# Two 128-column matmuls of a weight tile become one 256-column matmul in four blocks, and 8 more places get it

## The chip, the cores and the metric

The kernel runs on one NeuronCore of a Trainium2 chip. The metric is the device time of one execution in microseconds (us). Three runs of the kernel before took 982.0, 982.35 and 982.47 us, median 982.35 us. All tensors are float32. Five engines work side by side: TensorE (PE, matmuls, with its weight loads listed apart as PEld), VectorE (DVE), ScalarE (ACT), GpSimd (POOL) and SyncE (SP), which issues the DMAs.

## The reference

Three transformer layers on 256 tokens of width 1024: a latent-attention layer (0) and a chunked-attention layer (1), each with a SwiGLU feed-forward of width 2816, then a gated block with two attentions and a convolved feed-forward (2). Cut to what matters here:

```
for layer 0, 1:
    y = mixer(rms_norm(x))            # q, k, v products, softmax, @ w_o
    x = x + rms_norm(y)
    h = rms_norm(x)
    f = (silu(h @ w_gate) * (h @ w_up)) @ w_down
    x = x + rms_norm(f)
layer 2:
    proj = modulate(rms_norm(x)) @ w_in      # q, k, v of two attentions, gates
    mixed = (g_a * (oa @ w_br_moba) + g_b * (ob @ w_br_sb)) @ w_out
    x = x + gt_m * mixed
    u = conv(modulate(rms_norm(x)) @ w_up)
    x = x + gt_f * ((gelu(u_gate) * u_val) @ w_down)
    return rms_norm(x)
```

## The kernel before, in words

**Products.** Activations lie transposed: feature chunk k of 128 rows, 256 tokens as columns. Each 128x128 weight tile is multiplied with a 128x256 activation chunk. For accuracy every float32 operand is split into a high and a low part, both of type fp32r, and a product is three matmuls into the same 128x256 half of a PSUM bank: high weights by high activations (line 508), high weights by low activations (line 509), low weights by high activations (line 514). Each matmul is preceded on PE by the load of its own 128x128 weights. In `lead` (lines 528, 529, 535), which starts a stage while its activations are still being made, the high activations go first and the low ones after them.

**Weights.** SP brings pieces of 16 tiles (1 MB) into four buffers `raw`. ACT copies a piece to its high part `whi` (line 906), DVE subtracts that from the original and gives the low part `wlo` (line 1382). There are three `whi`/`wlo` buffers. PE's `weight` waits for the low part of a piece before its first use.

**Order.** Each engine's order is written out by hand as a program of its own; semaphores tie them. The stages are those of `STREAM`: `wa`, the latent products (`mla`), `wo0`, `gu0`, `dn0`, `wkv_v`, `wkv_k`, `wq1`, `wo1`, `gu1`, `dn1`, `win_v`, `win_k`, `win_q`, `win_g`, `wbr`, `wout`, `up2`, `dn2`. `gu` is gate and up of a feed-forward, `dn` its down product. `tiles` computes two output chunks at a time, n and n+1, over all k. Between stages lie the norms, which go through PE (sums of squares by a matmul with ones), ACT (logarithm, exponential) and DVE.

**The halved places.** At 29 places the third matmul of a product (line 514) is two matmuls of 128 columns instead (lines 511 and 512), each with its own load of the same weights. The table `HALVED` says where: in `tiles`, at k = 1 of chunk n, when n divides by the number in the table; and at k = 1 of the first chunk of each `dn` stage. That is 5 places each in `gu0`, `gu1` and `up2`, 4 in each `dn`, one in `wkv_k` and one in `win_k`.

Of the kernel before, what the change touches and what calls it, by code (L numbers as in the profile page):

```python
# [13 lines left out]
T = 256  # L14
P = 128
# [83 lines left out]
def _used_up(name, t):  # L99
# [3 lines left out]

AFTER = {"exp": ("scores", 5), "scale": ("exp", 4), "values": ("turn1", 3), "chunk": ("values", 2),
         "keep": ("sticks", 9), "sums": ("keep", 8), "stick": ("sums", 4)}
HALVED = {"gu0": 8, "gu1": 8, "up2": 8, "dn0": 2, "dn1": 2, "dn2": 2, "wkv_k": 8, "win_k": 8}
FREE = ("scale", "exp", "chunk", "keep", "stick")


# [196 lines left out]
def build(nc, a):  # L306
    ctx = ExitStack()
    with ctx:
# [177 lines left out]
        def tensor_program(e, counted):  # L486
# [10 lines left out]
            def weight(name, t, n=1):  # L497
# [4 lines left out]
                s, at = w % SPLIT, slice(c * P, (c + n) * P)  # L502
                return whi[s][:, at], wlo[s][:, at], w if c + n == PIECES[WEIGHTS[w]][3] else None

            def product(name, t, out, xh, xl, k, first, last, event=None, halves=False):

                hi, lo, used = weight(name, t)
                e.matmul(out, hi, xh[:, k, :], start=first, stop=False, skip_group_check=True)  # L508
                e.matmul(out, hi, xl[:, k, :], start=False, stop=False, skip_group_check=True)  # L509
                if halves:  # L510
                    e.matmul(out[:, 0:P], lo, xh[:, k, 0:P], start=False, stop=last, skip_group_check=True)
                    m = e.matmul(out[:, P:T], lo, xh[:, k, P:T], start=False, stop=last, skip_group_check=True)
                else:
                    m = e.matmul(out, lo, xh[:, k, :], start=False, stop=last, skip_group_check=True)  # L514
                if used is not None or event is not None:
                    m.then_inc(S.gemm.tick(("used", used), event), 1)

            def lead(name, m, nk, xh, xl, made, bs, by):

                for i, b in enumerate(bs):  # L520
                    take(b, by, (name, 2 * i))
                    bank_of[name, 2 * i] = b
                for k in range(nk):
                    q.wait_ge(S.xhi, (made, k))
                    for j in range(m):
                        out = banks[bs[j // 2]][:, (j % 2) * T:(j % 2 + 1) * T]
                        hi, lo, _ = weight(name, k * m + j)
                        e.matmul(out, hi, xh[:, k, :], start=k == 0 and j % 2 == 0, stop=False, skip_group_check=True)  # L528
                        e.matmul(out, lo, xh[:, k, :], start=False, stop=False, skip_group_check=True)  # L529
                    q.wait_ge(S.xlo, (made, k))  # L530
                    for j in range(m):
                        out = banks[bs[j // 2]][:, (j % 2) * T:(j % 2 + 1) * T]
                        hi, lo, used = weight(name, k * m + j)
                        event = (name, j - 1) if k == nk - 1 and j % 2 == 1 else None
                        last = e.matmul(out, hi, xl[:, k, :], start=False, stop=k == nk - 1, skip_group_check=True)  # L535
                        if used is not None or event is not None:
                            last.then_inc(S.gemm.tick(("used", used), event), 1)

            def tiles(name, n, m, nk, xh, xl, made, b, by, last=0, seven=None):


                out = take(b, by, (name, n + last))
                outs = [out[:, j * T:(j + 1) * T] for j in range(m)]
                bank_of[name, n] = b
                if seven is not None:
                    outs[1] = take(seven, by, (name, n + last))[:, 0:T]
                    bank_of[name, "seven"] = seven
                for j in range(m):
                    for k in range(nk):
                        q.wait_ge(S.xlo, (made, k))  # L550
                        event = (name, n) if j == m - 1 else (name, "six") if seven is not None else None
                        product(name, (n + j) * nk + k, outs[j], xh, xl, k, k == 0, k == nk - 1,
                                event if k == nk - 1 else None, name in HALVED and j == 0 and k == 1 and n % HALVED[name] == 0)

            def token_block(name, g, nk, xh, xl, k, tb):

# [111 lines left out]
            def out_chunk(name, t, xh, xl, made):  # L668

                k, j = t // 8, t % 8  # L670
                if k == 0 and j % 2 == 0:
                    take(j // 2, S.resid, (name, j + 1))
                    bank_of[name, j] = j // 2
                q.wait_ge(S.xlo, (made, "o", k))
                product(name, t, banks[j // 2][:, (j % 2) * T:(j % 2 + 1) * T], xh, xl, k, k == 0 and j % 2 == 0, k == 7,
                        (name, j - 1) if k == 7 and j % 2 == 1 else None)


            q.wait_ge(S.const, "ones")
# [133 lines left out]
            for step, i in _order2():  # L813
                if step in ("win_q", "win_g"):
                    n, k = i // 8, i % 8
                    if n % 2 == 0 and k == 0:
                        bank_of[step, n] = n // 2 % 3
                        take(n // 2 % 3, S.act_out, (step, n))
                    q.wait_ge(S.xlo, ("h4", k))
                    product(step, i, banks[n // 2 % 3][:, (n % 2) * T:(n % 2 + 1) * T], hh, hl, k, k == 0, k == 7,  # L820
                            (step, n - 1) if n % 2 == 1 and k == 7 else None)
                elif step == "scores":
                    q.wait_ge(S.act_out, ("win_k", i // 2 * 2))
                    q.wait_ge(S.act_out, ("win_q", i // 2 * 2))
                    scores("o2", i, half_parts(A2, i), (3, 4))
                elif step == "turn":
                    turn("o2", A2, *i, (5, 6)[i[1]])
                elif step == "sticks":
                    q.wait_ge(S.act_out, ("win_k", i // 2 * 2))
                    q.wait_ge(S.act_out, ("win_q", i // 2 * 2))  # L830
                    (heads,) = half_parts(A2, i)
                    pair_banks = []
                    for a in range(2):
                        b = 3 + 2 * (i % 2) + a
                        pair_banks.append(take(b, S.dve_tmp, ("least", i, a)))
                        bank_of["sticks", i, a] = b
                    for a, (x, y) in enumerate(heads):
                        e.matmul(pair_banks[a][:, 0:T], y[:, 0:P], x, start=True, stop=True, skip_group_check=True)
                    for a, (x, y) in enumerate(heads):
                        e.matmul(pair_banks[a][:, T:384], y[:, P:T], x[:, P:T], start=False, stop=True,  # L840
                                 skip_group_check=True).then_inc(S.attn.tick(("sticks", i, a)), 1)
                elif step == "sums":
                    for a in range(2):
                        bank, r = banks[bank_of["sticks", i, a]], A2.PT[i % 2][:, a, :]
                        q.wait_ge(S.past, ("keep", i, a))
                        e.matmul(bank[:, 0:T], tri[:, :], r[:, 0:T], start=False, stop=False, skip_group_check=True)
                        e.matmul(bank[:, P:T], negones[:, :], r[:, T:384], start=False, stop=False,
                                 skip_group_check=True)
                        e.matmul(bank[:, T:384], tri[:, :], r[:, T:384], start=False, stop=True,
                                 skip_group_check=True).then_inc(S.attn.tick(("sums", i, a)), 1)  # L850
                elif step == "values" and i < 4:
                    values("o2", A2, i, 64, A2.PT[i % 2], ("win_v", 0, 1), S.soft, ("o2", "turned", i, 1), 7)
                elif step == "values":
                    values("o2", A2, i, 64, A2.S[i % 2], ("win_v", 1, 1), S.past, ("stick", i, 1), 7)


            for n in range(8):
                bank_of["wbr", n] = (0, 1, 2, 3, 6, 7, 0, 1)[n]
                bank = take(bank_of["wbr", n], S.dve_tmp, ("gated", n))
                for b in range(2):  # L860
                    for k in range(4):
                        q.wait_ge(S.xlo, ("o2", "o", 4 * b + k))
                        product("wbr", n * 8 + b * 4 + k, bank[:, b * T:(b + 1) * T], A2.oh[:, 4 * b:4 * b + 4, :],
                                A2.ol[:, 4 * b:4 * b + 4, :], k, k == 0, k == 3,
                                ("wbr", n) if b == 1 and k == 3 else None)
            lead("wout", 4, 8, hh, hl, "mix", (4, 5), S.resid)
            for n in (4, 6):
                tiles("wout", n, 2, 8, hh, hl, "mix", (6, 7)[n // 2 - 2], S.resid, seven=3 if n == 6 else None)
# [1288 lines left out]
```

## Time and profile before

| | |
|---|---|
| median of three runs | 982.35 us (982.0 to 982.47) |
| span of the profiled execution, first to last instruction | 980.3 us |
| median above that span | 2.05 us |
| PE busy with matmuls | 958.4 us, 98% |
| PE busy with weight loads | 923.9 us, 94% |
| DVE busy | 720.6 us, 74% |
| ACT busy | 542.4 us, 55% |
| granted TensorE clock, mean over the span | 0.999 |
| HBM traffic | 197 GB/s over the span |

The page gives the span of the profiled execution and no device time of its own beside it; what lies around the span is read from the median of the other runs. A matmul is pipelined: its listed length (some 276 ns) is from the start of its reading to its modelled end, and the next one starts long before that. So the pace of PE is the distance from one start to the next, which the timeline gives to 10 ns and a window row gives as a mean: the window's length plus one matmul's length, divided by the count of matmuls that touch the window.

### The profile page before, as it was taken

Reading aid. Unit: us, or ns where it says so; the run is one execution under the profiler, and the core shown is the slowest. Engines: PE = TensorE matmul, PEld = TensorE weight load, DVE = VectorE, ACT = ScalarE, POOL = GpSimd, SP = SyncE. Lnnn points to the kernel's source line nnn. Section 1 sums busy time; section 2 is a strip of 40 time slices with the busy share of each in tenths; the row PEclk is TensorE's granted clock in tenths of the full one; section 3 lists DMA queues with packets and bytes.
Section 4 is the critical chain, followed back from the end, with each engine's and each line's share of the span. In section 5 each row is a group of like instructions: output and inputs, shape, how many; then the busy total and the mean of one; then the engine's idle time right before and its main releaser. Section 6 shows DMA issues by size and latency. Waiting matters only on the chain.

```text
span 980.3 us, 18888 instructions
## 1 busy us (share of the span) xinstructions
PE 958.4 (98%) x7971; PEld 923.9 (94%) x7971; DVE 720.6 (74%) x1340; ACT 542.4 (55%) x837; POOL 25.4 (3%) x54
## 2 busy tenths in 40 slices
PE   8999999999999999999999999999999999999997
PEld 8889999999998988899999997998999999999996
DVE  7965897777658777698879788555654879888653
ACT  7554664454447366565444545456755567666542
POOL 0300000000000000000000000000220000000000
PEclk9999999999999999999999999999999999999999
DMA  8536376766744734368767882653343545555621
GB/s 298 190 116 238 128 266 255 255 251 225 295 172 168 266 129 140 116 212 304 265 251 267 331 315 76 245 185 116 111 149 132 199 157 207 181 203 184 216 87 43
DMA packets 27588, 194.72 MB, mean 199 GB/s; under 512 B 3056, under 2 KB 3184, under 8 KB 4592
## 3 DMA queue, kind: packets, MB, share of 16 engines
q1 hardware_dynamic: 27504, 193.51, 54.7%
q8 instruction: 63, 1.03, 0.4%
q14 instruction: 21, 0.17, 0.0%
HBM read 192.45 MB, written 1.05 MB: 197 GB/s over the span
## 4 chain that ended last, share of the span: by engine, by line
PE 89%; ACT 4%; DVE 4%; issue 2%; DMA 1%; POOL 0%; SPq 0%; DVEq 0%; ACTq 0%
PE bank L508 25%; PE bank L509 24%; PE bank L514 23%; PE bank L639 2%; PE bank L665 2%; PE bank L569 2%; PE bank L563 2%; ACT s_whi L906 2%; PE bank L564 2%; PE bank L528 2%; PE bank L535 1%; PE bank L529 1%; PE bank L649 1%; DVE s_wlo L1382 1%; DMA s_xT<-in_xT 1%
## 5 line engine op out<-in xcount | busy, mean ns | idle before, releaser
L1382 DVE TENSOR_TENSOR s_wlo<-s_raw,s_whi 128x512 fp32r<-128x512 f32 (+1 forms) x364 | 372.3, 1065 | 138.1 <-ACT s_whi L906 137.9
L906 ACT ACTIVATE s_whi<-s_raw 128x1024 fp32r<-128x1024 f32 (+2 forms) x233 | 304.8, 1335 | 215.6 <-PE bank L514 205.9
L508 PE MATMUL bank<-s_hh,s_whi 128*128 128x256 f32 x1400 | 393.6, 281 | 1.1 <-DVE s_wlo L1382 0.7
L509 PE MATMUL bank<-s_hl,s_whi 128*128 128x256 f32 x1400 | 387.6, 277 | 0.0
L514 PE MATMUL bank<-s_hh,s_wlo 128*128 128x256 f32 x1383 | 382.8, 277 | 0.0
L508 PEld LDWEIGHTS bank<-s_hh,s_whi 128*128 128x128 f32 x1400 | 263.3, 188 | 6.9 <-issue 5.9
L509 PEld LDWEIGHTS bank<-s_hl,s_whi 128*128 128x128 f32 x1400 | 263.2, 188 | 0.1
L514 PEld LDWEIGHTS bank<-s_hh,s_wlo 128*128 128x128 f32 x1383 | 259.8, 188 | 0.0
L508 PE MATMUL bank<-s_ph,s_whi 128*128 128x256 f32 x528 | 146.4, 277 | 0.0
L509 PE MATMUL bank<-s_pl,s_whi 128*128 128x256 f32 x528 | 145.8, 276 | 0.0
L514 PE MATMUL bank<-s_ph,s_wlo 128*128 128x256 f32 x516 | 142.5, 276 | 0.0
L509 PEld LDWEIGHTS bank<-s_pl,s_whi 128*128 128x128 f32 x528 | 99.2, 188 | 0.0
L508 PEld LDWEIGHTS bank<-s_ph,s_whi 128*128 128x128 f32 x528 | 99.2, 188 | 0.0
L514 PEld LDWEIGHTS bank<-s_ph,s_wlo 128*128 128x128 f32 x516 | 96.9, 188 | 0.0
L1397 DVE CUSTOM_DVE_ANT_0 s_raw<-s_raw,s_adacc 128x1024 f32<-128x1024 f32 x48 | 56.7, 1219 | 0.0
L528 PE MATMUL bank<-s_hh,s_whi 128*128 128x256 f32 x160 | 39.8, 284 | 5.3 <-DVE s_wlo L1382 3.1
L529 PE MATMUL bank<-s_hh,s_wlo 128*128 128x256 f32 x160 | 39.1, 279 | 0.0
L508 PE MATMUL bank<-s_oh,s_whi 128*128 128x256 f32 x128 | 36.9, 288 | 0.6 <-DVE s_ol L1464 0.4
L1647 DVE TENSOR_TENSOR s_tmp<-bank,s_R 128x256 f32<-128x256 f32 x44 | 18.6, 422 | 25.3 <-PE bank L514 22.0
L528 PEld LDWEIGHTS bank<-s_hh,s_whi 128*128 128x128 f32 x160 | 30.2, 189 | 6.6 <-ACT s_hh L1022 2.2
L509 PE MATMUL bank<-s_ol,s_whi 128*128 128x256 f32 x128 | 35.8, 280 | 0.0
L514 PE MATMUL bank<-s_oh,s_wlo 128*128 128x256 f32 x128 | 35.8, 280 | 0.0
(238 smaller groups left out, 1285.3 us busy)
## 6 DMA issues: line engine op xcount, KB each, us to landing
s_raw<-in_gu SPq DMA_DIRECT2D x44, 1024.0 KB, 4.9
s_raw<-in_dn SPq DMA_DIRECT2D x33, 1024.0 KB, 4.9
s_raw<-in_wada SPq DMA_DIRECT2D x24, 1024.0 KB, 5.7
s_raw<-in_up SPq DMA_DIRECT2D x22, 1024.0 KB, 4.9
s_raw<-in_wo SPq DMA_DIRECT2D x8, 1024.0 KB, 4.9
s_raw<-in_win_g SPq DMA_DIRECT2D x8, 1024.0 KB, 4.9
s_raw<-in_mla SPq DMA_DIRECT2D x4, 1024.0 KB, 5.4
s_raw<-in_wkv_v SPq DMA_DIRECT2D x4, 1024.0 KB, 4.9
```

The lines of the kernel that those rows point to most:

```text
L508: e.matmul(out, hi, xh[:, k, :], start=first, stop=False, skip_group_check=True)
L509: e.matmul(out, hi, xl[:, k, :], start=False, stop=False, skip_group_check=True)
L514: m = e.matmul(out, lo, xh[:, k, :], start=False, stop=last, skip_group_check=True)
L528: e.matmul(out, hi, xh[:, k, :], start=k == 0 and j % 2 == 0, stop=False, skip_group_check=True)
L529: e.matmul(out, lo, xh[:, k, :], start=False, stop=False, skip_group_check=True)
L563: e.matmul(out, xh[:, k, xk], hi, start=k == 0, stop=False)
L564: e.matmul(out, xh[:, k, xk], lo, start=False, stop=False)
L569: m = e.matmul(out, xl[:, k, xk], hi, start=False, stop=k == nk - 1)
L639: m = e.matmul(pair_banks[a][:, cols_], x[:, blk * P:(blk + 1) * P], y[:, 0:rows], start=i == 0 and blk == 0, stop=last, skip_group_check= ...
L906: e.activation(whi[w % SPLIT][:, at], raw[p % RAW][:, at], ACT.Copy).then_inc(S.hi.tick((w, c0)), 1)
L1382: e.tensor_tensor(wlo[s][:, at], raw[p % RAW][:, at], whi[s][:, at].bitcast(F32), ALU.subtract).then_inc(S.lo.tick((i, j), (i, "all")), 1)
L1397: m = e.tensor_tensor_reduce(out=src, in0=src, in1=cact[:, :], scale=1.0, scalar=0.0, op0=ALU.mult, op1=ALU.add, accum_out=modv[:, j:j + 1])
```

## The change

It alters the matmuls of PE alone; no semaphore, DMA or instruction of another engine is added, removed or moved.

- At the 29 places the two 128-column matmuls become one matmul over all 256 columns. Its source (activations) and its target (PSUM) are both read through `turned_order`: 64 columns at a time, block 0, block 2, block 1, block 3. Every column still gets its own sum.
- Eight places are added that had one plain matmul: chunk n = 10 of `gu0`; weight tile 36 of `wo0`, 52 of `wo1`, 96 of `win_g`, 49 of `wbr`; and k = 1, j = 0 of the three leads of `gu1`, `wout` and `up2`, where the matmul with the low weights is the second one.

```
-HALVED = {"gu0": 8, "gu1": 8, "up2": 8, "dn0": 2, "dn1": 2, "dn2": 2, "wkv_k": 8, "win_k": 8}
+HALVED = {"gu0": (8, 10, 16, 24, 32, 40), "gu1": (8, 16, 24, 32, 40), "up2": (8, 16, 24, 32, 40),
+          "dn0": (0, 2, 4, 6), "dn1": (0, 2, 4, 6), "dn2": (0, 2, 4, 6), "wkv_k": (0,), "win_k": (0,)}
+HALVED_UNIT = {"wo0": (36,), "wo1": (52,), "win_g": (96,), "wbr": (49,)}
+HALVED_LEAD = ("gu1", "wout", "up2")
...
+            def turned_order(ap):
+
+                return ap.rearrange("p (a b c) -> p b a c", a=2, b=2)
...
                 if halves:
-                    e.matmul(out[:, 0:P], lo, xh[:, k, 0:P], start=False, stop=last, skip_group_check=True)
-                    m = e.matmul(out[:, P:T], lo, xh[:, k, P:T], start=False, stop=last, skip_group_check=True)
+                    m = e.matmul(turned_order(out), lo, turned_order(xh[:, k, :]), start=False, stop=last, skip_group_check=True)
...
-                        e.matmul(out, lo, xh[:, k, :], start=False, stop=False, skip_group_check=True)
+                        if name in HALVED_LEAD and k == 1 and j == 0:
+                            e.matmul(turned_order(out), lo, turned_order(xh[:, k, :]), start=False, stop=False,
+                                     skip_group_check=True)
+                        else:
+                            e.matmul(out, lo, xh[:, k, :], start=False, stop=False, skip_group_check=True)
...
-                                event if k == nk - 1 else None, name in HALVED and j == 0 and k == 1 and n % HALVED[name] == 0)
+                                event if k == nk - 1 else None, j == 0 and k == 1 and n in HALVED.get(name, ()))
```

On PE, in `gu0` at chunk n = 16 (152.2 us in the trace), before: `whi` and `wlo` are the weight parts, `hh` and `hl` the activation parts.

```order
970 L508 MATMUL bank1<-s_hh,s_whi0 128x256
971 L509 MATMUL bank1<-s_hl,s_whi0 128x256
972 L511 MATMUL bank1<-s_hh,s_wlo0 128x128
973 L512 MATMUL bank1<-s_hh,s_wlo0 128x128
974 L508 MATMUL bank1<-s_hh,s_whi0 128x256
975 L509 MATMUL bank1<-s_hl,s_whi0 128x256
976 L514 MATMUL bank1<-s_hh,s_wlo0 128x256
```

The same place on PE in the changed kernel:

```order
969 L515 MATMUL bank1<-s_hh,s_whi0 128x256
970 L516 MATMUL bank1<-s_hl,s_whi0 128x256
971 L518 MATMUL bank1<-s_hh,s_wlo0 128x2x2x64
972 L515 MATMUL bank1<-s_hh,s_whi0 128x256
973 L516 MATMUL bank1<-s_hl,s_whi0 128x256
974 L520 MATMUL bank1<-s_hh,s_wlo0 128x256
```

Two rows became one of a new form, 128x2x2x64; with it one weight load goes.

On PE, in the lead of `up2` at k = 1 (791.6 us in the trace), before:

```order
5830 L535 MATMUL bank2<-s_hl,s_whi0 128x256 x2
5831 L528 MATMUL bank1<-s_hh,s_whi0 128x256
5832 L529 MATMUL bank1<-s_hh,s_wlo0 128x256
5833 L528 MATMUL bank1<-s_hh,s_whi0 128x256
5834 L529 MATMUL bank1<-s_hh,s_wlo0 128x256
```

The same place on PE in the changed kernel:

```order
5810 L545 MATMUL bank2<-s_hl,s_whi0 128x256 x2
5811 L534 MATMUL bank1<-s_hh,s_whi0 128x256
5812 L536 MATMUL bank1<-s_hh,s_wlo0 128x2x2x64
5813 L534 MATMUL bank1<-s_hh,s_whi0 128x256
5814 L539 MATMUL bank1<-s_hh,s_wlo0 128x256
```

Here the count stays the same and one matmul takes the new form.

## Rows read from the trace of the kernel before

**Rows 1.** The page: span and busy times, then the chain that ended last.

```profile
span 980.3 us, 18888 instructions
PE 958.4 (98%) x7971; PEld 923.9 (94%) x7971; DVE 720.6 (74%) x1340; ACT 542.4 (55%) x837; POOL 25.4 (3%) x54
...
PE 89%; ACT 4%; DVE 4%; issue 2%; DMA 1%; POOL 0%; SPq 0%; DVEq 0%; ACTq 0%
```

**Rows 2.** Stretches of PE: window, its us, PE busy (count), clock, DMA share, GB/s.

```profile
91.20:100.90 9.70, 9.70 (x84) 1.00 1.00 391
135.30:152.10 16.80, 16.80 (x145) 1.00 0.90 320
401.30:405.10 3.80, 3.80 (x34) 1.00 0.00 0
411.80:427.10 15.30, 15.30 (x132) 1.00 0.32 112
791.60:813.20 21.60, 21.60 (x186) 1.00 0.43 157
153.30:174.00 20.70, 20.70 (x185) 1.00 0.65 235
435.30:456.30 21.00, 21.00 (x188) 1.00 0.90 318
152.70:289.00 136.30, 136.30 (x1203) 1.00 0.67 240
813.60:971.80 158.20, 158.20 (x1395) 1.00 0.46 161
316.90:346.10 29.20, 29.20 (x258) 1.00 0.75 281
434.80:592.80 158.00, 158.00 (x1395) 1.00 0.79 286
625.40:653.00 27.60, 27.60 (x245) 1.00 0.54 194
```

**Rows 3.** Timeline of PE around one halved place: start us, length us.

```profile
174.10 0.22 PE L511 MATMUL bank<-s_hh,s_wlo 128*128 128x128 f32 x1
174.16 0.28 PE L512 MATMUL bank<-s_hh,s_wlo 128*128 128x128 f32 x1
174.27 0.33 PE L508 MATMUL bank<-s_hh,s_whi 128*128 128x256 f32 x1
174.44 0.28 PE L509 MATMUL bank<-s_hl,s_whi 128*128 128x256 f32 x1
...
175.02 0.28 PE L508 MATMUL bank<-s_hh,s_whi 128*128 128x256 f32 x1
```

**Rows 4.** Timeline of DVE and PE at the end of the `gu1` lead.

```profile
426.07 2.28 DVE L1382 TENSOR_TENSOR s_wlo<-s_raw,s_whi 128x2048 fp32r<-128x2048 f32 x1
...
428.50 0.36 PE L508 MATMUL bank<-s_hh,s_whi 128*128 128x256 f32 x1 [0.67 <-DVE s_wlo L1382]
```

**Rows 5.** Timeline of ACT, DVE and PE in the `wbr` and `wout` stages.

```profile
756.45 0.36 PE L508 MATMUL bank<-s_oh,s_whi 128*128 128x256 f32 x1
...
757.67 0.42 ACT L1287 ACTIVATE s_hh<-s_tmp 128x256 fp32r<-128x256 f32 x1 [3.39 <-DVE s_tmp L1882]
757.99 1.90 ACT L906 ACTIVATE s_whi<-s_raw 128x2048 fp32r<-128x2048 f32 x1
...
754.01 2.29 DVE L1382 TENSOR_TENSOR s_wlo<-s_raw,s_whi 128x2048 fp32r<-128x2048 f32 x1 [0.96 <-ACT s_whi L906]
759.92 2.29 DVE L1382 TENSOR_TENSOR s_wlo<-s_raw,s_whi 128x2048 fp32r<-128x2048 f32 x1 [0.96 <-ACT s_whi L906]
765.84 2.29 DVE L1382 TENSOR_TENSOR s_wlo<-s_raw,s_whi 128x2048 fp32r<-128x2048 f32 x1 [0.95 <-ACT s_whi L906]
```

**Rows 6.** Timeline of DVE and PE in `gu0`, then at the start of `up2`.

```profile
132.17 2.28 DVE L1382 TENSOR_TENSOR s_wlo<-s_raw,s_whi 128x2048 fp32r<-128x2048 f32 x1
...
134.60 0.36 PE L508 MATMUL bank<-s_hh,s_whi 128*128 128x256 f32 x1
...
148.60 2.28 DVE L1382 TENSOR_TENSOR s_wlo<-s_raw,s_whi 128x2048 fp32r<-128x2048 f32 x1
...
157.22 0.28 PE L508 MATMUL bank<-s_hh,s_whi 128*128 128x256 f32 x1
...
797.13 4.50 DVE L1382 TENSOR_TENSOR s_wlo<-s_raw,s_whi 128x2048 fp32r<-128x2048 f32 x2 [1.32 <-ACT s_whi L906]
...
801.36 0.28 PE L508 MATMUL bank<-s_hh,s_whi 128*128 128x256 f32 x1
```

More of the change, by code:

```diff
@@ L675, in out_chunk @@
                 product(name, t, banks[j // 2][:, (j % 2) * T:(j % 2 + 1) * T], xh, xl, k, k == 0 and j % 2 == 0, k == 7,
-                        (name, j - 1) if k == 7 and j % 2 == 1 else None)
+                        (name, j - 1) if k == 7 and j % 2 == 1 else None, t in HALVED_UNIT[name])
             q.wait_ge(S.const, "ones")
@@ L820, in tensor_program @@
                     product(step, i, banks[n // 2 % 3][:, (n % 2) * T:(n % 2 + 1) * T], hh, hl, k, k == 0, k == 7,
-                            (step, n - 1) if n % 2 == 1 and k == 7 else None)
+                            (step, n - 1) if n % 2 == 1 and k == 7 else None, i in HALVED_UNIT.get(step, ()))
                 elif step == "scores":
@@ L864, in tensor_program @@
                                 A2.ol[:, 4 * b:4 * b + 4, :], k, k == 0, k == 3,
-                                ("wbr", n) if b == 1 and k == 3 else None)
+                                ("wbr", n) if b == 1 and k == 3 else None, n * 8 + b * 4 + k in HALVED_UNIT["wbr"])
             lead("wout", 4, 8, hh, hl, "mix", (4, 5), S.resid)
```

## The prediction

> **What bounds the kernel now.** I read the page first. PE is busy for 98% of the span and makes up 89% of the chain that ended last [rows 1], so the question is at what pace PE works. Its listed busy time cannot say that, since each matmul is listed with its whole pipelined length. I therefore asked for windows inside long runs without a wait, and took the distance from start to start: the window's length plus one matmul's length (0.28 us), over the count.
>
> Two paces come out [rows 2]. Window 153.30 to 174.00: (20.70 + 0.28) / 185 = 113.4 ns a matmul; 435.30 to 456.30: 21.28 / 188 = 113.2. Window 135.30 to 152.10: 17.08 / 145 = 117.8 ns; 791.60 to 813.20: 21.88 / 186 = 117.6; 411.80 to 427.10: 15.58 / 132 = 118.0. The instructions are of the same form, the granted clock is 1.00 (2.4 GHz) in all of them, and the DMA share does not separate them (0.90 and 0.43 at the slow pace, 0.65 and 0.90 at the fast). So PE has a fast pace of 113.4 ns and a slow one of 117.8, 4.4 ns or 4% apart, and keeps whichever it has. The slow one is entered after waits, and left at a wait or at a halved place: the window of `gu0` up to 152.10 is slow, the one behind its halved place is fast. This is what the timeline allows me to say; why a pace holds it doesn't show.
>
> The other engines bound only the starts of stages, where PE waits for a low weight part or for a norm.
>
> **The change part by part.**
>
> *1. The second matmul and its weight load go, at 29 places.* In a fast stretch the halved place runs from 174.10 to 175.02, 0.92 us for 8 steps [rows 3]. Without the extra matmul there would be 7 steps of 113.4 ns, 0.794 us. A halved place thus costs 0.126 us: one whole step of 113 ns, for a matmul costs a step whether it has 128 or 256 columns, and 13 ns in the five steps behind it, from 174.44 to 175.02 (5 steps in 0.58 against 0.567 us). The one at 129.4 us stands ahead of a wait: DVE's low part ends at 134.45 and PE goes on at 134.60 [rows 6], so its gain is lost there. 28 x 0.126 = 3.5 us.
>
> *2. What the new form costs by itself.* The trace has no matmul in blocks of 64. From below: nothing; it has 256 columns and one weight load, like its neighbours at 113.4 ns, and doing less than these is excluded, as the same count of columns is read. From above: the 0.126 us of the halved place, which also breaks the run of columns and loads weights twice. I take the small disturbance seen behind the halved place, 13 ns, because the nearest row is the plain 256-column matmul and a break in a run of columns is what the halved place has in common with the new form. It counts at 28 old and 5 new places: 33 x 0.013 = 0.4 us.
>
> The row first: the two-part place shows that breaking 256 columns once costs 13 ns beside the extra step. The Trainium skill ("Advanced Engine Details and Errata", section "PSUM Cachelines") says that any non-contiguous access pattern slows matmuls significantly, and that pairs of elements should be contiguous for best throughput. By its first sentence part 1 would give back most of what it gains; by its second a pattern that breaks only every 64 elements costs next to nothing. It gives no figure, and no row here decides; the rival of a dear form below is what its first sentence would make here.
>
> *3. The pace behind the eight new places.* If the new form resets the pace as the halved place did, the slow stretch behind each becomes fast. By the windows there stand behind them [rows 2]: `wo0` 9.98 / 0.1178, 84 touched, 82 whole; `gu0` 143; `wo1` 32; lead of `up2` 183. Together 440 x 4.4 ns = 1.94 us. The first two and the last end in work of PE or in a norm that hangs on PE's last sum, so this gain reaches the end. Weights are there: in `gu0` the part ready at 150.88 is used at 157.22; in `up2` the one ready by 801.63 is the later of two, and the first of them, ready by about 799.4, is used at 801.36 [rows 6].
>
> The lead of `gu1` has 130 slow matmuls, 0.57 us, but behind it PE waits 0.67 us for a low part that DVE ends at 428.35 after its own run of norm work [rows 4]. PE would wait longer: nothing gained. In `wbr` and `wout` the slow steps are covered too: DVE's low parts come every 5.91 us (754.01, 759.92, 765.84), in a ring of DVE and ACT that doesn't pass through PE (low part, DVE's mix, ACT's copy at 757.67, high part at 757.99, next low part) [rows 5], while PE needs 48 x 0.1178 = 5.65 us for a piece even when slow. Nothing gained. Tile 96 of `win_g` comes at about 727 us, eight matmuls ahead of the next attention step, and is counted at nothing.
>
> *4. The pace at the old places.* 24 of the 29 stand in fast stretches, where only part 1 matters. Of the others three stand in slow ones with a long run behind: `gu0` at 152.2, `wkv_k` at 316.6, `up2` at 813.3. If the new form resets there too, nothing changes.
>
> Sum: -3.5 + 0.4 - 1.9 = -5.0 us. The profiled execution's span of 980.3 us would be 975.3; with the 2.05 us between span and median of the runs, 977.3 us. What becomes late next: nothing in the feed-forward stages, where low parts are ready some 5 us ahead; at the starts of stages the waits for low parts stay where they are.
>
> **The rivals.**
>
> *The new form doesn't reset the pace* (the side of slower). It runs like a plain matmul, with one weight load after the other, and the two quick 128-column steps (174.10 to 174.16) that may be what shifts the pace are gone. Then the slow stretches run on: from 152.70, from 813.60 and from 316.90 the windows touch 1203 + 1395 + 258 = 2856 matmuls, less 16 second halves and some 10 at the edges 2830 [rows 2]. 2830 x 4.4 ns = 12.5 us, against 29 x 0.126 = 3.6 saved: +8.9, 991.2 us. It decides from 3600 / 4.4 = 820 slow matmuls on. For it: every step out of the slow pace that I see was a halved place or a wait. Against it: the pace is left after disturbances of different kinds (a wait, the sums of a norm), so it seems to take little.
>
> *It resets, but is dear.* If one new-form matmul costs as much as the halved place, the old places gain nothing and the five useful new ones cost 0.6: 982.35 - 1.9 + 0.6 = 981.0 us.
>
> *It also throws PE from the fast pace into the slow one.* Then the stretches from 434.80 and 625.40 turn slow as well, some 1640 more matmuls [rows 2], 4470 in all: 19.7 - 3.6 = +16.1, 998.4 us. For it: a disturbance by a wait ends in either pace. Against it: all halved places in fast stretches ended fast.
>
> *The paces are dealt anew.* All waits shift by fractions of a us, and each can end in either pace; stretches with no place in them (before `wo0`, `wq1`, `win_g` from 730 to 750 us with some 170 matmuls) may turn slow or fast, 0.7 us apiece. If this or a later wait for DVE takes half of the gain: about 980 us.
>
> **How the numbers follow.** 0.64 for the forecast (977.3, own range 974.8 to 979.6), 0.12 for the dear form, 0.12 for no reset, 0.04 for the throw into the slow pace, 0.08 for half the gain. A gap of 0.2% (2.0 us) is about what a measurement of this kernel can tell from no change, so faster means below 980.4, slower above 984.3. Faster: nearly all of the forecast's 0.64, over half of the 0.08 and a quarter of the dear form (0.126 us is its upper end), 0.71. Same: the rest of these, 0.13. Slower: no reset and the throw, 0.16. The range from 974.6 to 983.0 holds the forecast, the dear form and the half gain, 0.8 together; no reset stays outside.
>
> **What would show it.** The page: 29 matmuls fewer, 7942. The timeline of PE at 152 us: after the new form the next starts come at 0.11 to 0.12 us with no 0.17 step, and the windows behind it give 113.4 ns. The windows after the new places in `wo0`, `gu0`, `wo1` and the lead of `up2` give 113.4 and not 117.8. The wait of PE for the low part after the lead of `gu1` grows from 0.67 to about 1.2 us, and the distance of low parts in `wout` stays at 5.91. I am wrong if windows behind a new-form matmul give 117.8, or if the step at that matmul is much over 0.13 us.

## The result, and the profile after

The changed kernel took 992.33 us (median of four runs: 987.30, 991.61, 993.04, 998.16), the kernel before 982.41 us (982.0 to 985.99) beside it. The ratio is 1.0096, 95% interval 1.0072 to 1.0119: slower by 1%, where 977.3 us and faster had been forecast. The rival "no reset" had 991.2 us. The spread of the four runs, 11 us, is part of the result.

The profile below is of the slowest of the four, 998.16 us, so it shows the loss at its largest. The page of the changed kernel, the lines that answer to [rows 1]:

```profile
span 994.4 us, 18830 instructions
PE 971.9 (98%) x7942; PEld 937.4 (94%) x7942; DVE 720.8 (72%) x1340; ACT 542.1 (55%) x837; POOL 25.4 (3%) x54
...
PE 92%; DVE 3%; ACT 3%; issue 1%; DMA 1%; POOL 0%; SPq 0%; DVEq 0%; ACTq 0%
```

The 29 matmuls and weight loads are gone, PE's listed busy time is 13.5 us longer all the same, and the other engines do the same work in the same time. So the matmuls that are left go at another pace. The windows of PE (window, its us, busy and count, clock, DMA share, GB/s), which answer to [rows 2]:

```profile
91.20:100.90 9.70, 9.70 (x83) 1.00 1.02 391
135.30:152.10 16.80, 16.80 (x145) 1.00 0.92 319
153.30:174.00 20.70, 20.70 (x178) 1.00 0.65 235
152.70:289.00 136.30, 136.30 (x1160) 1.00 0.66 237
320.90:346.10 25.20, 25.20 (x225) 1.00 0.77 287
404.90:409.00 4.10, 4.10 (x37) 1.00 0.00 0
434.80:600.00 165.20, 165.20 (x1405) 1.00 0.77 278
801.00:822.00 21.00, 21.00 (x181) 1.00 0.42 153
813.60:971.80 158.20, 158.20 (x1346) 1.00 0.49 172
```

Window 153.30 to 174.00 now holds 178 matmuls instead of 185: (20.70 + 0.28) / 178 = 117.9 ns, the slow pace, behind the place that had ended it. The windows 152.70 to 289.00, 434.80 to 600.00 and 813.60 to 971.80 give 117.7, 117.8 and 117.7 ns: the three long stretches, `gu0` with `dn0`, `gu1` with `dn1`, `up2` with `dn2`, are slow from end to end. In the kernel before, the second of them was fast from its start, and the other two from the halved places at 152.2 and 813.3 us on. The short stretches in `wo0`, `wo1` and the lead of `up2` are slow as well, 120.2, 118.4 and 117.6 ns (the first two windows are so short that an edge counts). Of the stretches shown only `wkv_k`, 320.90 to 346.10, is fast, 113.2 ns.

PE around the turned matmul at chunk n = 16 of `gu0`, the place shown in the order above (start us, length us), which answers to [rows 3]:

```profile
152.00 0.28 PE L516 MATMUL bank<-s_hl,s_whi 128*128 128x256 f32 x1
152.12 0.28 PE L518 MATMUL bank<-s_hh,s_wlo 128*128 128x256 f32 x1
152.24 0.28 PE L515 MATMUL bank<-s_hh,s_whi 128*128 128x256 f32 x1
152.36 0.28 PE L516 MATMUL bank<-s_hl,s_whi 128*128 128x256 f32 x1
152.47 0.28 PE L520 MATMUL bank<-s_hh,s_wlo 128*128 128x256 f32 x1
```

Line 518 starts 0.12 us after its neighbour and the next one 0.12 us after it. In this trace the turned matmul does nothing: it costs nothing and changes nothing. PE comes to 31 of the 37 places at the slow pace and leaves each of them at the slow pace; it comes to the other six fast, or going over to fast, and leaves them fast.

I counted the slow steps in both traces: of some 7000 distances of 105 to 126 ns from one start to the next, taken in groups of up to nine, about 1160 go at the slow pace in the kernel before and about 5030 in the changed one. That is 3870 x 4.4 ns = 17.0 us more, less 29 x 0.126 = 3.7 us for the matmuls taken out, and PE's idle time (span less busy time, 22.5 against 21.9 us) is 0.6 us longer: +13.9 us. The two spans are 14.1 us apart (994.4 - 980.3).

### The profile page after: what moved, and what is told of

It reads as the page before. It is cut to its first block, busy times and chain, and to the rows that moved or that the text cites. A ratio compares the mean times of both kernels' runs of the same rounds, so it can differ in the third digit from the quotient of the medians.

```text
span 994.4 us, 18830 instructions
## 1 busy us (share of the span) xinstructions
PE 971.9 (98%) x7942; PEld 937.4 (94%) x7942; DVE 720.8 (72%) x1340; ACT 542.1 (55%) x837; POOL 25.4 (3%) x54
## 4 chain that ended last, share of the span: by engine, by line
PE 92%; DVE 3%; ACT 3%; issue 1%; DMA 1%; POOL 0%; SPq 0%; DVEq 0%; ACTq 0%
PE bank L515 25%; PE bank L516 25%; PE bank L520 24%; PE bank L649 2%; PE bank L675 2%; PE bank L534 2%; PE bank L579 2%; PE bank L545 2%; PE bank L573 2%; PE bank L574 2%; PE bank L539 2%; PE bank L659 1%; ACT s_whi L916 1%; DVE s_wlo L1392 1%; DMA s_xT<-in_xT 1%
## 5 line engine op out<-in xcount | busy, mean ns | idle before, releaser
L516 PE MATMUL bank<-s_hl,s_whi 128*128 128x256 f32 x1400 | 391.9, 280 | 0.0
L516 PE MATMUL bank<-s_pl,s_whi 128*128 128x256 f32 x528 | 148.5, 281 | 0.0
L515 PE MATMUL bank<-s_ph,s_whi 128*128 128x256 f32 x528 | 148.5, 281 | 0.0
L520 PE MATMUL bank<-s_ph,s_wlo 128*128 128x256 f32 x516 | 145.1, 281 | 0.0
L1943 DVE SCALAR_TENSOR_TENSOR s_tmp<-bank,s_cols,s_tmp 128x255 f32<-128x255 f32 (+1 forms) x44 | 21.2, 482 | 20.5 <-ACT s_tmp L1336 19.7
```

The lines of the kernel that those rows point to most:

```text
L1943: e.scalar_tensor_tensor(out=v[:, shift:T], in0=bank[:, 0:T - shift], scalar=col(name, n), in1=v[:, shift:T], op0=ALU.mult, op1=ALU.add)
```

## The experiments

Theory from here on: a wait deals the pace, fast or slow, anew in each execution; PE keeps it until the next wait, or other work of PE such as a norm's sums or attention, or until a halved place; and the turned form is a plain matmul. Rivals: the turned form itself, or the eight new places, make PE slow. The first four kernels ran on one chip beside the kernel before (982.99 us there), the last four on another (983.84 us). Each time below is the median of all runs of a kernel; a ratio is given where the times are tight.

**The halved form at all 37 places.** The change's list of places with the old form:

```
-                    m = e.matmul(turned_order(out), lo, turned_order(xh[:, k, :]), ...)
+                    e.matmul(out[:, 0:P], lo, xh[:, k, 0:P], ...)
+                    m = e.matmul(out[:, P:T], lo, xh[:, k, P:T], ...)
```

> The changed kernel with the old form at all 37 places: two matmuls of 128 columns instead of one in four blocks. Theory (the turned form does nothing; only the halved form takes PE out of the slow pace): the stretches of gu0, gu1, the dn stages and up2 run at 113.4 ns again, all halved places cost 0.126 us, and the eight new ones end the slow stretches behind them in wo0, gu0, wo1 and the up2 lead: 982.4 + 8 x 0.126 - 1.9, about 981.4 us (980.5 to 982.5). Rival (the slower time of the changed kernel comes from the eight new places, wherever they stand): it stays at 987 us or more.

982.8 us (981.21 to 983.67, 11 runs), ratio 0.9994 (0.9986 to 1.0003): no change from before, and tight. So the eight new places do no harm; the form is what differs. It had been expected 0.9 us under the kernel before (1.9 saved, 1.0 spent) and is 0.2 us under it. My reading, which no run tests by itself: the stretches that were slow in the profile before are not all slow in every execution, so ending them is worth less on average, and eight more places cost 1.0 us always. The ten profiles of this case bear it out in part. Ahead of their places, `wo0` and `wo1` were slow in all ten, `gu0` in five, the lead of `up2` in three. Weighted so, the 440 matmuls give (82 + 32 + 143/2 + 183 x 0.3) x 4.4 ns, an estimate of 1.1 us saved for 1.0 spent.

**No turned and no halved form.** All tables empty, and none in the `dn` stages.

```
+HALVED = {}
+HALVED_UNIT = {"wo0": (), "wo1": (), "win_g": (), "wbr": ()}
+HALVED_LEAD = ()
```

> The changed kernel with plain 256-column matmuls at all 37 places: no turned and no halved form anywhere. Theory (turned is the same as plain): the same times as the changed kernel, 987 to 998 us with the same wide spread from run to run, and slow stretches of over a thousand matmuls at 117.8 ns. Rival (the turned form itself slows PE or keeps it slow): 978.8 us, the kernel before less 29 x 0.126 us, and tight.

986.45 us, 12 runs: 979.14, 979.25, 980.03, 980.29, 980.65; 986.15, 986.75, 987.52, 987.60; 991.42, 993.16; 999.95. The times come in steps. The run that was profiled took 979.14 us, and its three long stretches were all fast (windows, columns as above):

```profile
137.00:287.00 150.00, 150.00 (x1326) 1.00 0.71 254
430.00:590.00 160.00, 160.00 (x1414) 1.00 0.80 289
790.00:967.00 177.00, 177.00 (x1564) 1.00 0.48 165
```

That is 113.3, 113.4 and 113.4 ns over more than 1300, 1400 and 1500 matmuls without any halved place: a pace holds by itself. A slow draw costs 1343 x 4.4 = 5.9 us in the first, 1439 x 4.4 = 6.3 in the second, 1583 x 4.4 = 7.0 in the third. No slow stretch is 979 to 981, one is 985 to 988, two are 991 to 993, three 998 to 1000: the steps that were measured. The same code gave both 979 and 1000 us. The granted clock doesn't tell the runs apart: its mean over the span was 0.996 in the fastest and in the slowest.

Not every stop deals anew, though: `wo0` and `wo1`, which follow an attention stage, start slow in all ten profiles, `win_g` behind its last attention step in nine. The long stretches are the ones that come out either way.

**The turned form at the 29 old places alone.** `HALVED` with the chunks of the kernel before, the other two tables empty.

> The turned form at the 29 old places alone, plain at the eight new ones. Theory: as the changed kernel, 987 to 998 us. Rival (the new places do the harm): below the kernel before, 978.8 us.

987.02 us, 12 runs: 979.55, 980.11, 982.92; 985.43, 985.93, 986.66, 987.39; 990.53, 991.45, 992.64; 998.59, 999.51. The same ladder; the run of 982.92 us is the profiled one, with the three long stretches fast and, among the slow short ones, `win_k` and the lead of `gu0`, which the kernel before had fast. In that profile too no turned place changes the pace. The rival that the turned form makes PE slow falls, as three runs are as fast as the plain kernel's best; the rival that the new places do so falls too.

**The halved form at 8 places, each just behind a wait.**

```
+HALVED = {"gu0": (10,), "gu1": (6,), "wkv_k": (0,), "win_k": (0,)}
+HALVED_UNIT = {"wo0": (36,), "wo1": (52,), "win_g": (101,), "wbr": ()}
+HALVED_LEAD = ("up2",)
```

None in the `dn` stages.

> The halved form at 8 places alone, each a few matmuls behind the wait that starts a long run: wo0 36, gu0 10, wkv_k 0, wo1 52, gu1 6, win_k 0, win_g 101, lead of up2; none in the dn stages. Theory (a pace holds until the next wait, and one halved place behind the wait is enough): all long runs at 113.4 ns; 21 places fewer save 2.6 us, ended slow stretches (wo0, gu0, wo1, win_g, up2: some 610 matmuls x 4.4 ns) 2.7 us: about 977.0 us (976 to 978.5), tight. Rival (the pace falls back by itself in a long run, so that the repeated places are needed): windows late in gu0, dn0, gu1, dn1, up2, dn2 give 117.8 ns and the time is 983 us or more.

979.36 us (978.13 to 979.47, 5 runs), ratio 0.9961 (0.9949 to 0.9973): faster than both kernels, and tight. It missed 977.0 by 2.4 us: 0.6 us of it is the kernel before, slower on that chip, and the rest I put to the recovered stretches, which had been taken as slow in every execution. By the counts above they would be worth some 1.7 us instead of 2.7, an estimate that accounts for about half of the rest. Windows of its profile, in `win_g`/`wbr` and the long stretches:

```profile
137.00:287.00 150.00, 150.00 (x1326) 1.00 0.71 252
430.00:590.00 160.00, 160.00 (x1414) 1.00 0.79 287
728.20:747.40 19.20, 19.20 (x172) 1.00 0.33 111
```

and its timeline of PE at tile 101 of `win_g`:

```profile
727.50 0.28 PE L514 MATMUL bank<-s_hh,s_whi 128*128 128x256 f32 x1
727.62 0.28 PE L515 MATMUL bank<-s_hl,s_whi 128*128 128x256 f32 x1
727.74 0.22 PE L517 MATMUL bank<-s_hh,s_wlo 128*128 128x128 f32 x1
727.80 0.28 PE L518 MATMUL bank<-s_hh,s_wlo 128*128 128x128 f32 x1
727.91 0.33 PE L514 MATMUL bank<-s_hh,s_whi 128*128 128x256 f32 x1
728.08 0.28 PE L515 MATMUL bank<-s_hl,s_whi 128*128 128x256 f32 x1
```

Steps of 0.12 us ahead of it, then 0.06, 0.11, 0.17, and the window behind it holds 172 matmuls in 19.20 us, 113.3 ns. In the plain, the changed and the turned-29 kernel this stretch was slow. Repeated places in the long stretches of the kernel before were not needed.

What in the halved form resets the pace, that is, brings PE from the slow pace to the fast one? Three kernels change the form at these same 8 places.

**The low-weight matmul twice over all 256 columns.**

```
+                    e.matmul(out, lo, xh[:, k, :], ...)
+                    m = e.matmul(out, lo, xh[:, k, :], ...)
```

The low product is then added twice at these places, so the output differs by that; the time is what this kernel is for.

> At the 8 places of the kernel with 8 halved places the low-weight matmul is issued twice over all 256 columns instead of in two halves, so the low product is added twice there (the output differs by that). It keeps the extra weight load and the extra step and takes away the two short steps. Theory (the short matmuls reset the pace, because they take the matmul start off its place behind the weight load): no reset; the stretches behind wo0 36, wo1 52 and win_g 101, slow before them in every profile so far, stay at 117.8 ns, and the times spread over 980 to 1000 us like the plain kernel's. Rival (the extra weight load resets it): they turn to 113.4 ns and the time is about 979.4 us, tight.

986.28 us (979.97 to 999.31, 10 runs), the ladder again. Windows in `wo0`, `gu1` with `dn1`, `win_g`/`wbr`, `up2` with `dn2`:

```profile
92.50:102.50 10.00, 10.00 (x87) 1.00 0.98 392
...
431.00:598.00 167.00, 167.00 (x1420) 1.00 0.76 277
736.00:756.00 20.00, 20.00 (x172) 1.00 0.30 107
798.00:982.00 184.00, 184.00 (x1564) 1.00 0.46 158
```

All of them are 117.8 to 118.2 ns, behind a place with an extra step and an extra weight load. So neither of these resets the pace. What is left of the halved form is that its matmuls are short.

**Cut at column 64, then at column 192.**

```
+                    e.matmul(out[:, 0:64], lo, xh[:, k, 0:64], ...)
+                    m = e.matmul(out[:, 64:T], lo, xh[:, k, 64:T], ...)
```

> The 8 halved places cut at column 64: matmuls of 64 and 192 columns. Theory: one short matmul is enough, the pace is reset as with the halves, each place costs one step of 113 ns: 979.4 us (978 to 980.5), tight. Rival (only equal halves do it): slow stretches stay behind wo0 36, wo1 52, win_g 101, and the times spread up to 990 us and more.

> The same places cut at column 192: 192 columns first, then 64. Theory: a short step anywhere resets, 979.4 us, tight. Rival (what counts is how early the second matmul follows the first, 57 ns with halves, 85 here): no reset in some places, wide spread.

Cut at 64: 979.24 us (978.34 to 979.86, 4 runs), ratio 0.9953 (0.9937 to 0.997), like the halves. Cut at 192: 983.39 us (978.60 to 992.95, 10 runs): the times spread as the rival said, and a short second matmul isn't enough. Windows behind tile 36 of `wo0` and tile 101 of `win_g`, for the cut at 64:

```profile
92.80:101.40 8.60, 8.60 (x78) 1.00 1.00 400
729.00:748.20 19.20, 19.20 (x171) 1.00 0.32 111
```

and for the cut at 192:

```profile
91.60:100.50 8.90, 8.90 (x78) 1.00 0.97 395
728.00:747.80 19.80, 19.80 (x170) 1.00 0.32 108
```

The timelines of PE at tile 101 of `win_g`, first for the cut at 64, then for the cut at 192:

```profile
728.62 0.20 PE L517 MATMUL bank<-s_hh,s_wlo 128*128 128x64 f32 x1
728.65 0.33 PE L518 MATMUL bank<-s_hh,s_wlo 128*128 128x192 f32 x1
728.82 0.30 PE L514 MATMUL bank<-s_hh,s_whi 128*128 128x256 f32 x1
...
727.49 0.25 PE L517 MATMUL bank<-s_hh,s_wlo 128*128 128x192 f32 x1
727.58 0.22 PE L518 MATMUL bank<-s_hh,s_wlo 128*128 128x64 f32 x1
727.63 0.36 PE L514 MATMUL bank<-s_hh,s_whi 128*128 128x256 f32 x1
727.84 0.28 PE L515 MATMUL bank<-s_hl,s_whi 128*128 128x256 f32 x1
```

With the cut at 64 the windows give 113.8 ns in `wo0` and 113.9 in `win_g`, with the cut at 192 they give 117.7 and 118.1. In the slow stretches the second matmul follows the first after some 61 ns (halves), 32 ns (cut at 64), 89 ns (cut at 192) and 118 ns (twice); the first two ended the slow pace at each of the four places that stood in a slow stretch in their profile, the last at none of five. Cut at 192, three of four stayed slow (`wo0`, `wo1`, `win_g`); in `win_k` PE went over to the fast pace five matmuls later, by the place or by itself (without a working place it did so there in the changed kernel). Whether the width of the first matmul decides or the delay to the second, these cuts don't separate.

**Pairs of columns in turn.** The changed kernel with `turned_order` by pairs:

```
-                return ap.rearrange("p (a b c) -> p b a c", a=2, b=2)
+                return ap.rearrange("p (a b c) -> p b a c", a=64, b=2)
```

> The changed kernel with its 37 turned matmuls reading and writing pairs of columns in turn: pairs 0, 2, 4, ... then 1, 3, 5, ..., so every second column breaks the run, in the source and in PSUM. Theory (a break between pairs is free, as a break between blocks of 64 was): steps of 113 to 118 ns at those matmuls and times spread like the changed kernel's, 979 to 1000 us. Rival (any pattern that is not contiguous slows a matmul significantly): the step at such a matmul is 150 ns or more, and 37 of them cost 1.4 us or more; being longer it might also reset the pace.

994.96 us (993.79 to 996.07, 4 runs), ratio 1.0113 (1.0098 to 1.0128), and tight. The timeline of PE at two places of `gu0`, 153.24 and 175.13 us:

```profile
153.12 0.28 PE L516 MATMUL bank<-s_hl,s_whi 128*128 128x256 f32 x1
153.24 0.39 PE L518 MATMUL bank<-s_hh,s_wlo 128*128 128x256 f32 x1
153.45 0.30 PE L515 MATMUL bank<-s_hh,s_whi 128*128 128x256 f32 x1
153.59 0.28 PE L516 MATMUL bank<-s_hl,s_whi 128*128 128x256 f32 x1
...
175.13 0.39 PE L518 MATMUL bank<-s_hh,s_wlo 128*128 128x256 f32 x1
175.35 0.30 PE L515 MATMUL bank<-s_hh,s_whi 128*128 128x256 f32 x1
```

Windows between the places of `gu0` in the same profile:

```profile
136.70:153.10 16.40, 16.40 (x141) 1.00 0.89 322
153.80:174.90 21.10, 21.10 (x188) 1.00 0.64 236
175.70:197.60 21.90, 21.90 (x188) 1.00 0.67 239
198.40:219.50 21.10, 21.10 (x188) 1.00 0.66 236
```

The step at such a matmul is 0.21 us instead of 0.11 and the next 0.14, together 0.13 us more per place. And it turns the pace over: 118.3, 113.7, 118.0, 113.7 ns in four stretches one behind the other, and so at all places of the long stretches in that profile. The place in the lead of `wout`, at 772.80 us, is an exception: PE is slow ahead of it and behind it. That fixes the time: 979.2 + 37 x 0.13 + half of three slow stretches (9.6) = 993.6 us.

## Why the prediction was wrong

- **The two paces, their size and that they hold between waits**: right. 113.4 and 117.8 ns came back in every profile, at 1300 to 1600 matmuls in a row.
- **Part 1, a halved place costs 0.126 us, 3.5 us in all**: right. The plain kernel's five runs with all long stretches fast lie at 979.1 to 980.7 us, the kernel before at 983.0 beside them, and in the traces a halved place is 0.127 us longer than plain steps.
- **Part 2, the new form costs 13 ns**: it cost nothing; its step was 114 ns where PE went at 113.4, and 117 to 120 where it went at 117.8. The size was small either way. The Trainium skill's two sentences ("Advanced Engine Details and Errata", section "PSUM Cachelines") can now be set beside two measurements. Blocks of 64 columns cost nothing, against the first sentence, which speaks of any non-contiguous pattern; there the measurement decides. Pairs of columns in turn took 0.21 us against 0.11. That agrees with the first sentence, and shows that contiguous pairs, which the second asks for, are not enough for full speed here. The source and the target were both read in pairs, and which of them costs the time was not separated.
- **Parts 3 and 4, "if the new form resets the pace as the halved place did"**: this is the step that failed. The new form leaves the pace as it finds it, whichever of the two that is: slow stayed slow at 31 of 31 places, and the three long stretches ran at 117.7 to 117.8 ns instead of 113.4. I had given 0.64 to it on the argument that the pace is left after disturbances of different kinds; but every disturbance in the trace had been a wait, other work such as a norm's sums, or a short matmul, and the new form has none of these. The twice-issued matmul shows the same: an extra step is no disturbance. Part 4 also counted `wkv_k` among the slow stretches. In the trace of the kernel before PE was already going over to the fast pace ahead of that place, and in the changed kernel, where the place does nothing, that stretch went at 113.2 ns. Part 3's 1.9 us was too large by itself: the halved form, which does reset the pace, came 0.2 us under the kernel before with these eight places where 0.9 us were expected.
- **The pace behind a wait** was the second error. I took slow and fast stretches from one profiled execution as a property of the kernel. The long ones are drawn anew: over the 28 runs of the changed, the plain and the turned-29 kernel some 35 of 84 long stretches were slow, read from each run's step of the ladder (the three profiles among them agree with their steps). The rival's 991.2 us came near the median by luck, a cancelling of two faults: it counted three slow stretches, `wkv_k` among them, and left `gu1` with `dn1` out. The expected time of the changed kernel is 979.2 + 0.42 x 19.2 = 987.3 us; its first four runs drew two slow stretches of three on average.
- **What is covered by waits**: the waits stayed where they were put. The wait for a low part behind the lead of `gu1` was 0.67 us and is now 0.82 us, not the 1.2 us that the prediction named, with the lead fast at first and slow at its end in this execution. The low parts in `wout` still came every 5.9 us.

```profile
432.56 0.36 PE L515 MATMUL bank<-s_hh,s_whi 128*128 128x256 f32 x1 [0.82 <-DVE s_wlo L1392]
```

What the halved places of the kernel before were doing is clear now: they cost 3.7 us and held the three long stretches at the fast pace, which is worth 0.42 x 19.2 = 8 us on average, an estimate from the ladder, and takes the spread from 20 us down to 5.

Open is why PE has two paces. The trace shows that each holds itself, that a wait can end in either, that a first matmul of 64 or 128 columns leads from slow to fast and that one of 192 doesn't; it doesn't show the mechanism. Nor was a reset found that costs less than one step.

## What to carry to other kernels

Measure the pace of PE from start to start, in windows without a wait, before anything else: a few per cent can hide in a stretch in which no engine waits. Where there are two paces, cut one matmul in two, the first part 64 or 128 columns wide, once behind each wait that opens a long run, and not at regular distances; here 8 places (979.36 us) did better than 29 (982.99) or 37 (982.8). And when the times of a kernel come in steps, one profile shows one draw: compare sets of runs, and ask of each stretch what the others drew.

## What was not expected of the hardware

- Matmuls of 256 columns with a weight load each ran at 113.4 or at 117.8 ns from start to start, at the same granted clock (1.00), and kept the pace for up to 1583 matmuls, slow in the changed kernel and fast in the plain one.
- The same program took 979.1 and 999.95 us on one core of one chip.
- A matmul with its columns in four blocks of 64, in source and target, ran like a plain one; in alternate pairs of columns it took 0.21 us and turned the pace over at every place of the long stretches.
- A second matmul of 128 or 192 columns started 61 or 32 ns after a first of 128 or 64, while its own weight load takes 188 ns as listed.
